# Delta phase of a two-block layer: the tokens' projection ahead of the decay projection, three half groups behind each opening step, and each input waited for where it is used

## What is computed

```python
xn = _rms(x, norm_gain)
proj = einsum('bsd,dp->bsp', xn, w_in)
qkv_a = silu(causal_dwconv(proj[..., :1536], conv_w))
q_a, k_a = l2n(q), l2n(k)                       # 4 heads of 128
beta = sigmoid(proj[..., A_Z1:A_B1])            # 4 columns: one per head
g = -exp(a_log) * softplus(proj[..., A_B1:A_A1] + dt_bias)   # 4 columns
# per chunk of 64 tokens: gc = cumsum(g), decay = exp(gc_i - gc_j),
# solve (I + beta*kk*decay) [u, w] = rhs, then scan over the chunks:
v_new = u_c - w_c @ state
o = qd_c @ state + qk_c @ v_new
state = state * exp(gc_end) + kd_c.T @ v_new
# the other columns of proj (z_a, and q, k, v, z of the second branch)
# are used by the later phases
```

## Time and profile before

| | us |
|---|---|
| median of 3 timed runs | 2778.96 |
| lowest, highest | 2775.7, 2780.8 |
| the profiled execution | 2784.54 |
| its span in the profile | 2782.6 |
| mean granted TensorE clock over the span | 0.968 of full speed |
| start of the delta phase (first instruction) | 170.38 |
| start of the next phase | 685.56 |

### The profile page before, as it was taken

One profiled execution on the slowest core, in us unless ns is written; L12 is line 12 of the kernel. 1 busy time (PEld: TensorE's weight loads), 2 busy tenths in 40 slices (PEclk: granted clock), 3 DMA queues, 4 the chain that ended last, 5 costly groups with the idle time before them and its releaser, 6 DMA issues. The chain is left out here.

```text
span 2782.6 us, 36583 instructions
## 1 busy us (share of the span) xinstructions
PE 2615.7 (94%) x14702; PEld 2245.0 (81%) x14702; DVE 1263.3 (45%) x1770; ACT 938.4 (34%) x1549; POOL 352.8 (13%) x450
## 2 busy tenths in 40 slices
PE   8969999998799998999997989889999999999999
PEld 6849999997588886888886877767888888778877
DVE  6523444442466764543136858454233222323452
ACT  4223322221456652123115767532212111222331
POOL 1002232220332320001012223010000000000000
PEclk9979999999799998999998989989999999999999
DMA  4222121112333215443323211163222222355532
GB/s 144 86 75 82 53 77 49 53 43 64 103 117 92 74 56 185 148 137 101 122 97 102 56 41 39 35 215 92 68 69 76 71 81 68 112 180 171 189 102 80
DMA packets 215503, 264.71 MB, mean 95 GB/s; under 512 B 46852, under 2 KB 147844, under 8 KB 215336
## 3 DMA queue, kind: packets, MB, share of 16 engines
q1 hardware_dynamic: 215336, 262.38, 29.6%
HBM read 185.11 MB, written 77.22 MB: 94 GB/s over the span
## 5 line engine op out<-in xcount | busy, mean ns | idle before, releaser
L3801 PE MATMUL ffn_up_acc<-mixed_hi,ffn_ring_hi 128*128 128x512 f32 x704 | 274.9, 390 | 2.5 <-DVE mixed_lo L2922 2.5
L3801 PE MATMUL ffn_up_acc<-mixed_hi,ffn_ring_lo 128*128 128x512 f32 x704 | 274.6, 390 | 0.0
L3801 PE MATMUL ffn_up_acc<-mixed_lo,ffn_ring_hi 128*128 128x512 f32 x704 | 274.5, 390 | 0.0
L1379 PE MATMUL delta_acc<-delta_w_hi,xn_hi 128*128 128x256 f32 x640 | 192.0, 300 | 2.9 <-DVE delta_w_lo L1333 2.9
L1381 PE MATMUL delta_acc<-delta_w_hi,xn_lo 128*128 128x256 f32 x640 | 181.5, 284 | 0.0
L1380 PE MATMUL delta_acc<-delta_w_lo,xn_hi 128*128 128x256 f32 x640 | 181.4, 283 | 0.0
L3801 PEld LDWEIGHTS ffn_up_acc<-mixed_hi,ffn_ring_hi 128*128 128x128 f32 x704 | 132.6, 188 | 30.2 <-issue 2.9
L3801 PEld LDWEIGHTS ffn_up_acc<-mixed_lo,ffn_ring_hi 128*128 128x128 f32 x704 | 132.6, 188 | 27.5
L3801 PEld LDWEIGHTS ffn_up_acc<-mixed_hi,ffn_ring_lo 128*128 128x128 f32 x704 | 132.5, 188 | 27.5
L4060 DVE TENSOR_TENSOR ffn_feed_lo<-ffn_feed_raw,ffn_feed_hi 128x1536 fp32r<-128x1536 f32 x44 | 77.4, 1759 | 148.1 <-ACT ffn_feed_hi L4052 148.0
L3771 DVE TENSOR_SCALAR ffn_conv<-ffn_padded,ffn_taps 128x1024 f32<-128x1024 f32 x22 | 16.6, 753 | 276.3 <-ACT ffn_padded L3752 276.3
(11 more groups left out here) (444 smaller groups left out, 6449.7 us busy)
## 6 DMA issues: line engine op xcount, KB each, us to landing
ffn_feed_raw<-in_w_down SPq DMA_DIRECT2D x44, 512.0 KB, 3.9
ffn_ring_raw<-in_w_gate SPq DMA_DIRECT2D x11, 1024.0 KB, 5.3
ffn_ring_raw<-in_w_up SPq DMA_DIRECT2D x11, 1024.0 KB, 5.8
scratch_act_t<-ffn_silu SPq DMA_DIRECT2D x22, 512.0 KB, 2.7
ffn_feed_raw<-scratch_act_t SPq DMA_DIRECT2D x44, 256.0 KB, 3.0
delta_w_raw<-in_w_in SPq DMA_DIRECT2D x20, 512.0 KB, 4.0
scratch_projected<-delta_out SPq DMA_DIRECT2D x80, 128.0 KB, 1.7
stick_g_raw<-in_w_in SPq DMA_DIRECT2D x16, 512.0 KB, 4.6
```

The costliest lines, as they stand in the source:

```text
L1379: nc.tensor.matmul(acc, self.hi[:, k, tok], w_hi, start=(k == 0), stop=False, skip_group_check=True)
L3801: last = nc.tensor.matmul(self.acc[s][:, br, cols], weight[:, k, ch], part[:, k, cols], start=(k == 0 and first), stop=(k == 7 and weight ...
```

## The change

- Stage 0 has one more step at its head. In it SP issues the loads of `ba_raw` and the two rows; the other engines do nothing (POOL sets its constant). The masks and the first tile's inputs are issued in the step after it.
- The semaphore `inputs` becomes three: `w_in`, `rows_in`, `mask_in`. Each is waited for by the engine that uses the data, at the use.
- The plan begins with that step, then four half groups; each of the four opening steps is followed by three half groups. The remaining 146 steps of stage 3 are spread over the 140 rounds of the tiles.

```diff
-        self.inputs, self.xt_in, self.stored = ph.sem("inputs"), ph.sem("xt_in"), ph.sem2("stored")
+        self.w_in, self.rows_in, self.mask_in = (ph.sem(n) for n in ("w_in", "rows_in", "mask_in"))
+        self.xt_in, self.stored = ph.sem("xt_in"), ph.sem2("stored")
...
     def sync(self, sp):
...
-        sp.dma_start(d.w_raw[:], d.w_beta_a.rearrange("(k p) n -> p k n", p=P)).then_inc(d.inputs, 16)
-        sp.dma_start(d.a_row[:], row(d.a_log)).then_inc(d.inputs, 16)
-        sp.dma_start(d.dt_row[:], row(d.dt_bias)).then_inc(d.inputs, 16)
-        sp.dma_start(d.mask[:], d.masks.rearrange("l p n -> p l n")).then_inc(d.inputs, 16)
+        sp.dma_start(d.w_raw[:], d.w_beta_a.rearrange("(k p) n -> p k n", p=P)).then_inc(d.w_in, 16)
+        sp.dma_start(d.a_row[:], row(d.a_log)).then_inc(d.rows_in, 16)
+        sp.dma_start(d.dt_row[:], row(d.dt_bias)).then_inc(d.rows_in, 16)
+        yield
+        sp.dma_start(d.mask[:], d.masks.rearrange("l p n -> p l n")).then_inc(d.mask_in, 16)
         load(0)
...
     def scalar(self, act):
...
-        act.wait_ge(d.inputs, 64)
+        yield
+        act.wait_ge(d.w_in, 16)
         pre.done(nc.scalar.activation(d.w_hi[:], d.w_raw[:], ACT.Copy), "w_hi")
...
+        act.wait_ge(d.rows_in, 32)
         pre.done(nc.scalar.activation(d.exp_a[:], d.a_row[:], ACT.Exp), "exp_a")
...
     def vector(self, dve):
...
+        yield
         pre.wait(dve, "w_hi", 1)
...
         pre.wait(dve, "kept", 1)
+        dve.wait_ge(d.rows_in, 32)
...
     def gpsimd(self, pool):
...
         pre.done(nc.gpsimd.memset(d.half[:], -0.5), "half")
+        yield
...
     def tensor(self, pe):
...
+        yield
         pre.wait(pe, "w_lo", 1)
...
         pre.wait(pe, "g", 1)
+        pe.wait_ge(d.mask_in, 16)
...
 def delta_plan(others):
...
-    plan, given = [], 0
-    rounds = Delta.OPENING + Delta.STEPS * (TT + 2)
+    ahead, each = 4, 3
+    plan, given = [0] + [3] * ahead, ahead
+    for i in range(Delta.OPENING):
+        plan += [0] + [3] * each
+        given += each
+    first, rounds = given, Delta.STEPS * (TT + 2)
     for i in range(rounds):
-        t = (i - Delta.OPENING) // Delta.STEPS if i >= Delta.OPENING else -1
+        t = i // Delta.STEPS
...
-        want = others * (i + 1) // rounds
+        want = first + (others - first) * (i + 1) // rounds
```

## The result

The changed kernel has a median of 2784.56 us in 12 runs, against 2778.02 us of the kernel before in 12 runs: ratio 1.002, 95% interval 1.0011 to 1.0029. It is slower by 5.6 us on that ratio (3 to 8), by 6.5 us between the two medians. The forecast was 2773.9 us with a range of 2770.5 to 2779.5.

A forecast was written before the change was run, and what follows sets the result against it. TensorE work was taken to bound the tile rounds, with pause and half clock as losses in the opening. Opening 6.6 us less, tile rounds 1.5 more: 2778.96 - 5.1 = 2773.9 us, range 2770.5 to 2779.5.

The forecast's parts named there:

- The opening: Delta phase before the tile rounds: 6.6 us less apart from the twelve moved half groups, 4.8 of it the clock's fall.
- Start 179.4: First token matmul on TensorE in the opening: at 179.4 us, bounds 178.1 and 180.8, no earlier than before.
- projection from 188.7: Decay projection on TensorE: starts at 188.7 us, after four half groups and a new pause of 0.85 us.
- first q turn 218.4: End of the opening: TensorE's first turn of q comes near 218.4 us (201.1 + 17.3).
- no drop of the clock: Opening on TensorE: clock stays at 1.00 from about 185 us on, without a fall.
- no wait for g: End of the opening: a chain to g of about 8 us is covered by six half groups, 8.7 us, on TensorE.
- Tile 0: First tile: about 1.1 us of new TensorE idle ahead of the turn of kn.
- Tile rounds: Rounds after the opening: 1.5 us more together, from kn in tile 0, shifted waits ahead of upper and small holes.
- a drop behind a pause of 2.9 us: Old opening on TensorE: clock fell to half after this pause; its absence after the change makes 4.8 of 6.6 us.
- The slower one: Rival, tile rounds bound by their chain: each half group taken away leaves a 1.44 us hole; 2782.5 to 2791.1 us, chance 0.06.
- The rule of the Trainium skill that was weighed: Old opening: the clock's fall is absent in some timed runs; by it the gain is 0.3 us instead of 5.1.

The follow-up runs named there:

- e3: The kernel before, with VectorE making upper for the next tile at step 13 instead of step 0: 2778.07 us against 2779.33 before.
- e11: The kernel before, with upper for the next tile made directly behind VectorE's copy of w: 2775.26 us against 2777.54 before.
- e1: The changed kernel with some token weight splits moved out of the last three rounds before a tile, half groups per round untouched: 2779.41 us against 2779.33 before.
- e2: The changed kernel, with VectorE making upper for the next tile at step 13 instead of step 0: 2780.17 us against 2779.33 before.
- e6: The changed kernel, with upper for the next tile made directly behind VectorE's copy of w: 2771.37 us against 2778.55 before.
- e9: The changed kernel with one added wait: POOL starts its product of mt and a mask only after VectorE has made upper: 2773.23 us against 2778.55 before.
- e5: The change's three semaphores and waits at the use, with the plan of the kernel before: 2774.40 us against 2779.33 before.
- e8: The change's waits with the plan of the kernel before, and upper made behind the copy of w: 2770.78 us against 2778.55 before.

## Why the prediction was wrong

- **The opening was right.** Start 179.4, measured 179.86; projection from 188.7, measured 188.93 after a pause of 0.65 us; first q turn 218.4, measured 218.72; no drop of the clock, no wait for g. 6.6 us were forecast and 6.4 came. That the two agree so closely is in part luck, since 4.8 of the 6.6 us are one profile's fall of the clock. From the first load to the first q turn the old opening took 37.3 us in the profile of before, but 35.3 and 35.0 in e3 and e11; the new one took 47.2 to 48.3 in its five profiles (the changed kernel, e1, e2, e6, e9). By the means of these it gains 5.4 us, by the runs of e6 and e11 about 5.
- **Tile 0** was right: 1.1 us for kn, measured 0.94.
- **The step that failed is "Tile rounds".** It read that waits ahead of upper move with the token steps, but sized the move as "once instead of twice (1.1 less), against one weight split that now falls there (0.9 more)". Measured: 6.5 us more (10.8 instead of 4.3), since five of eight tiles begin behind a split in steps 11 to 13 and two of those waits are 2.4 us. I had looked only at the last round. Even there the count was off: copies in step 13 stand ahead of two tiles in both kernels (1 and 2 before, 5 and 8 after), and the wait behind the one at tile 8 is 2.18 us. The chain begins at the product w in step 12, so everything VectorE does from there counts; and it was already 0.22 us too long at most tiles of before, which I took for small change where it said that no slack was left. The step's items also add up to 1.3 us and not to the 1.5 of the text; that moves the forecast by 0.2 us and changes nothing.
- **Durations:** I used 1.2 us for the split and gave the two operations on upper no length; the trace of before already had 1.67 us (at 389.03, above) for an operation that takes 0.69 elsewhere. e9 shows why.
- **The clock in the rounds** was not in the sum: 5.1 us. I had weighed a drop behind a pause of 2.9 us, and did not ask what the clock would do if a longest wait of 1.4 us grew towards it. With 6.5 and 5.1 us more the tile rounds cost 12.5 us (0.9 of it for kn), where 1.5 was forecast.
- **The rivals.** The slower one had the right place, the tile rounds, and the wrong mechanism: not holes for missing half groups (e1 keeps their number and loses 6 us of the waits). The rule of the Trainium skill that was weighed ("TensorE: Matmul & The Clock Gate", What's actually happening: the number of slow matmuls differs from run to run of the same kernel) could not be put to the test as such, since every profile here is of another kernel. What the profiles show goes the same way: behind the same 2.88 us pause the clock was 0.50 for 10.2 us in two (before, e5), for 6.8 us in two (e3, e11) and not at all in one (e8), and of two equal waits in e2 one was followed by a drop.

The timed medians follow the phase lengths only within some 3 us (e1 is 10.0 us shorter in the phase than the changed kernel, 7 in the runs); which part of that is the scatter of the clock in single profiles stays open.

## What to carry to other kernels

When a plan is shifted by a number of steps, list what every engine's queue holds at each tight place of the other stages before and after the shift, not only at the place that is edited: here the shift alone cost 12.5 us in the profile where the edit gained 6.4. A wait of 0.2 us in most tiles meant here that a chain was just covered: what was put into it showed in full, and three waits that grew past 2 us cost the clock as well. Start a chain's last operations directly behind what releases them, ahead of work that can wait.

## What the runs showed of the hardware

- A VectorE product of two SBUF operands (128x512 f32) takes 0.69 us alone and up to 1.77 us beside POOL's products; the two POOL products beside it took 3.94 us instead of 2.53. The 128x1024 split went from 1.22 to 1.62 us. With POOL's products held back by one wait (e9) the subtraction took 0.69 us at all eight tiles, the mask product 0.68 to 0.93.
- Behind five of six pauses of TensorE of 2.17 to 2.42 us in otherwise full work, the granted clock was 0.50 for 3.4 us; behind none of the shorter pauses in the rounds (up to 1.84 us, in e9).
